# Third mixer: the Gelu of the compressed features moved three beats back, a one-column exponent behind it, the second layer one beat back

## Chip, cores and metric

One core of one Trainium2 chip. The metric is the device time of one execution in microseconds (us), lower is better. Five engines run programs of their own and meet only through semaphores: TensorE (PE in the profile, its weight loads PEld), VectorE (DVE), ScalarE (ACT), GpSimd (POOL) and SyncE (SP, which issues most of the DMAs).

## The reference, cut to what matters

Three layers on a sequence of 256 tokens with 1024 features: two layers of one kind (gated feed-forward, mixer, gated feed-forward), then one of another kind (mixer, feed-forward). The change lies in the mixer of the last one. It has two branches, a chunked mLSTM and an attention with three parts (compressed, selected and window keys). The compressed part reduces keys and values to 15 blocks by a small two-layer network:

```python
def compress_blocks(kv, pe, w1, w2):
    ...
    blk = kv[:, :, idx] + pe
    flat = blk.reshape(B, G, ncmp, CMP_LEN * dh)
    return jax.nn.gelu(flat @ w1, approximate=False) @ w2
...
    kcmp = compress_blocks(kc_t, cmp_k_pe, cmp_k_w1, cmp_k_w2)
    vcmp = compress_blocks(vc_t, cmp_v_pe, cmp_v_w1, cmp_v_w2)
...
        pc = masked_softmax(jnp.einsum('bghqd,bgnd->bghqn', qb, kc) * scale, cmask)
        o_cmp = jnp.einsum('bghqn,bgnd->bghqd', pc.astype(vc.dtype), vc)
```

The other two parts are ordinary softmax attention over 256 keys; with 8 heads they make 16 jobs, taken as 8 pairs.

## The kernel before

Everything is one straight program per engine, written out by hand. Weights stream from HBM through a ring of 8 raw buffers. ScalarE copies each weight tile into a high part (`whi`, line 1380), VectorE subtracts to get the low part (`wlo`, line 1989), and TensorE multiplies high and low parts separately to keep float32 accuracy; these products are most of the work.

The mixer of the last layer (`mixer2`, one function of that name in each engine's program) puts its small work between the big products. A counter, the beat, goes up after each block of big products; every engine has a function `tick` that raises its own counter and says which small steps are due at that beat. Nothing keeps the engines at the same beat but the semaphores, and each engine works strictly in the order of its program. Beats 31 to 38 lie between the blocks of the value projection of the mLSTM (tiles Mmv0, Mmv2, Mmv4, Mmv6, two beats each), beats 39 to 46 between those of the next projection (Mmo0 to Mmo6). On TensorE each of these blocks is lines 770, 771 and 775. Ahead of every second beat ScalarE and VectorE split the tiles that come next (`ahead`); how many tiles ahead is a table (`HI_LEAD`: two tiles, Mmo0 and Mmo2, fall due on ScalarE ahead of beat 35).

The steps around the change, with their lines:

- Attention pair 0 (the 16 jobs' first two) runs its scores at beat 29, its probabilities are turned at beats 33 and 34 (TensorE `turn_p`, line 1040; ScalarE copies each turned tile out of the one PSUM bank that they share, `turned_p`, line 1609, and the next turn waits for that copy). Pair 1 has its scores at beat 35 (TensorE line 1027), the row maxima on VectorE (lines 2234, 2235 and 2241) and four exponents on ScalarE at beat 35 (lines 1601 and 1602), and is turned at beats 39 and 40.
- The compressed part has steps of its own in `compressed`. TensorE step 0 (beat 31, line 1227) turns the first layer's sums, and ScalarE's step 1 applies Gelu to them (line 1810, out: `hc`, semaphore `c_hc`). TensorE step 1 (lines 1233 and 1236) is the second layer; it waits for `c_hc` and raises `c_w2`. ScalarE step 2 copies the results out in three pieces (lines 1680, 1681, 1816); it waits for `c_w2` and for two buffers that GpSimd clears (`vz`, line 2809 the second), and raises `c_kv` to 3. TensorE step 2 (line 1242, beat 36) waits for `c_kv` 3 and repeats the values for VectorE (line 2452). Step 3 on TensorE is at beat 38, line 1248; ScalarE's copy of the finished value projection is line 1942.
- GpSimd runs the mLSTM's small convolutions (lines 2790, 2793, 2795); ScalarE takes a Tanh of each when it is done (`conv_end`, line 1829, beats 32, 36, 40, 44).

An activation function needs its table in ScalarE. Where the next function is not in the table that is loaded, the compiled program has an ACT_TABLE_LOAD ahead of the instruction, under the same line number. Line 1534 is a one-column Gelu that an earlier author put ahead of the last feed-forward; it writes one column of `small` that nobody reads.

Of the kernel before, what the change touches and what calls it, by code (L numbers as in the profile page):

```python
# [10 lines left out]
ACT = mybir.ActivationFunctionType  # L11
# [404 lines left out]
def build_program(nc, x_in, wstream, gains, const_in, par_in, out, cat, pat, plan, addends):  # L416
# [3 lines left out]
    with ExitStack() as ctx:  # L420
        def sb(name, cols, dt=F32, parts=P):
            return ctx.enter_context(nc.sbuf_tensor(name, [parts, cols], dt))
# [17 lines left out]
        small = sb("small", 560)  # L440
# [7 lines left out]
        mhalf = small[:, 160:176]  # L448
# [250 lines left out]
        def pe_program(E):  # L699
            e = E.e  # L700
# [478 lines left out]
            def mixer2(s):  # L1179
                js = jobs2()  # L1180
                beat = 0

                def turn_k(a, first):
                    bk, dup = side[a], arena[:, a * 1024:a * 1024 + 1024]
                    if first:
                        E.wait_ge("x", 4 * (s - 1) + a + 1)
                        E.wait_ge("rp_add", 8 + a + 1)
                        turn4([dup[:, (2 + i) * P:(3 + i) * P] for i in range(4)], bk).then_inc(sem["kT_t"], 1)
                    else:
                        E.wait_ge("k3_ev", 2 * a + 2)  # L1190
                        E.wait_ge("kT_ev", a + 1)
                        turn4([dup[:, j * P:(j + 1) * P] for j in (0, 1, 6, 7)], bk).then_inc(sem["kT_t"], 1)

                def turn_q(a):
                    E.wait_ge("rp_add", 10 + a + 1)
                    E.wait_ge("kc2_ev", 4 * a + 4)
                    turn4([ro[:, a * 512 + c * P:a * 512 + c * P + P] for c in range(4)], side[a]).then_inc(sem["qkt_t"], 1)
# [23 lines left out]
                def compressed(step):  # L1221
                    b = side[3] if step < 4 else side[2]
                    if step == 0:
                        E.wait_ge("c_part", 1)
                        E.wait_ge("c_fold", 1)
                        for i in range(4):
                            ins = e.matmul(b[:, i * 30:i * 30 + 30], hpart[:, i * P:i * P + P], fold[:, 0:30], start=True, stop=True)
                        ins.then_inc(sem["c_hT"], 1)
                    if step == 1:
                        E.wait_ge("c_hc", 1)  # L1230
                        E.wait_ge("ld_p", 16)
                        for hb_ in range(2):
                            e.matmul(b[:, 0:30], PR("kw2")[:, hb_ * P:hb_ * P + P], hc[:, hb_ * 30:hb_ * 30 + 30], start=hb_ == 0, stop=hb_ == 1)
                        for g in range(2):
                            for hb_ in range(2):
                                ins = e.matmul(b[0:15, 64 + g * 64:128 + g * 64], hc[:, (2 + hb_) * 30 + g * 15:(2 + hb_) * 30 + g * 15 + 15],
                                               PR("vw2")[:, hb_ * P:hb_ * P + 64], start=hb_ == 0, stop=hb_ == 1)
                        ins.then_inc(sem["c_w2"], 1)
                    if step == 2:
                        E.wait_ge("c_kv", 3)  # L1240
                        for g in range(2):
                            ins = e.matmul(b[:, 256:320], C("rep")[:, g * P:g * P + P], vcs[:, g * 64:g * 64 + 64], start=g == 0, stop=g == 1)
                        ins.then_inc(sem["c_rep"], 1)
                    if step == 3:
                        E.wait_ge("c_v", 1)
                        for a in range(2):
                            for c in range(4):
                                ins = e.matmul(b[:, (a * 4 + c) * 32:(a * 4 + c) * 32 + 30], qT2[:, c * S + a * P:c * S + a * P + P],
                                               kcT[:, c // 2 * 30:c // 2 * 30 + 30], start=True, stop=True)
                        ins.then_inc(sem["c_sc"], 1)  # L1250
                    if step == 4:
                        E.wait_ge("c_s", 11)
                        E.wait_ge("pT_ev", 20)
                        for a in range(2):
                            ins = e.transpose(b[:, a * P:a * P + P], Pc[:, a * P:a * P + P], ident)
                        ins.then_inc(sem["c_pT"], 1)
# [46 lines left out]
                def tick():  # L1303
                    nonlocal beat
                    beat += 1
                    if 10 <= beat <= 13:
                        turn_k(beat % 2, beat < 12)
                    if beat in (24, 25):
                        turn_q(beat - 24)
                    if beat == 16:  # L1310
                        gate_rows()
                    attention(2, beat, 29, js, before)
                    if beat in (31, 34, 36, 38, 44):
                        compressed((31, 34, 36, 38, 44).index(beat))
                    if beat in range(ML, ML + 24, 6):
                        mlstm_scores((beat - ML) // 6)
                    if beat in range(ML + 4, ML + 28, 6):
                        mlstm_out((beat - ML - 4) // 6)
                    if beat in (ML + 28, ML + 30):
                        mlstm_turn((beat - ML - 28) // 2)  # L1320
# [35 lines left out]
        def act_program(E):  # L1356
            e = E.e
# [410 lines left out]
            def mixer2(s):  # L1768
                js = jobs2()
                beat = 0  # L1770
# [31 lines left out]
                def compressed(step):  # L1802
                    b = side[3] if step < 3 else side[2]
                    if step == 0:
                        E.wait_ge("tile", DONE["Mvw13"])
                        E.wait_ge("X", 8)
                        e.activation(hpart, side[3][:, :], ACT.Copy).then_inc(sem["c_part"], 1)
                    if step == 1:
                        E.wait_ge("c_hT", 1)
                        e.activation(hc, b[:, 0:120], ACT.Gelu).then_inc(sem["c_hc"], 1)  # L1810
                    if step == 2:
                        E.wait_ge("c_w2", 1)
                        E.wait_ge("vz", 2)
                        split_heads("c_kv", [kcT.rearrange("p (g hp n) -> p hp g n", g=2, hp=2)[:, hp] for hp in range(2)],
                                    b[:, 0:30].rearrange("p (g n) -> p g n", g=2))
                        e.activation(vcs[0:15, :], b[0:15, 64:192], ACT.Copy).then_inc(sem["c_kv"], 1)
                    if step == 3:
                        E.wait_ge("c_s", 5)
                        p3 = Pc.rearrange("p (r n) -> p r n", n=16)[:, :, 0:15]
                        e.activation(p3, p3, ACT.Exp).then_inc(sem["c_exp"], 1)  # L1820
                    if step == 4:
                        E.wait_ge("c_pT", 1)
                        e.activation(PcT, b[:, 0:S], ACT.Copy).then_inc(sem["c_pTe"], 1)
# [33 lines left out]
                def tick():  # L1857
                    nonlocal beat
                    beat += 1
                    if 10 <= beat <= 13:  # L1860
                        turned_k(beat % 2, beat < 12)
                    if beat == 18:
                        logf()
                    if beat in (24, 25):
                        turned_q(beat - 24)
                    if beat == 26:
                        exp_m()
                    if beat in CONV:
                        conv_end(CONV.index(beat))
                    if beat == 28:  # L1870
                        compressed(0)
                    attention(2, beat, 29, js)
                    if beat in (31, 34):
                        compressed((31, 34).index(beat) + 1)
                    if beat == 40:
                        compressed(3)
                    if beat == 44:
                        compressed(4)
                    if beat == ML + 1:
                        mlstm_exp(0)  # L1880
                    if beat in range(ML + 6, ML + 24, 6):
                        mlstm_exp((beat - ML) // 6)
                    if beat in (ML + 6, ML + 12, ML + 18, ML + 22):
                        mlstm_squares((ML + 6, ML + 12, ML + 18, ML + 22).index(beat))
                    if beat in (ML + 28, ML + 30):
                        mlstm_turned((beat - ML - 28) // 2)
# [1123 lines left out]
```

## Time and profile before

| | |
|---|---|
| median of 3 runs | 1405.89 us (1405.52 to 1406.15) |
| the profiled execution's own time | 1405.38 us |
| its span in the trace | 1403.6 us |
| TensorE busy | 1398.1 us |
| VectorE busy | 1087.4 us |
| ScalarE busy | 861.8 us |
| GpSimd busy | 229.0 us |

The span is from the first to the last instruction of the profiled execution; its own time has some 1.8 us around that. Busy times overlap between engines. Line numbers (L1810) are those of the kernel before.

### The profile page before, as it was taken

The numbers are of one execution on the slowest core, as the hardware profiler recorded it, in microseconds if no ns is written. First come the engines' busy times: TensorE is split into PE (matmuls) and PEld (weight loads), VectorE is DVE, ScalarE is ACT, GpSimd is POOL, SyncE is SP. The second block draws the span as 40 slices with busy tenths as digits, with TensorE's granted clock in tenths as the row PEclk, the third lists the DMA queues.
The fourth block names the chain that finished last, engine by engine and source line by source line (L and its number), as shares of the span: only waits on it lengthen the run. The fifth ranks groups of instructions, "written<-read, shape, count | busy, mean of one in ns | idle before, by whom it ended". The sixth has DMA issues, their size and how long they took to land.

```text
span 1403.6 us, 20147 instructions
## 1 busy us (share of the span) xinstructions
PE 1398.1 (100%) x7616; PEld 1194.2 (85%) x7616; DVE 1087.4 (77%) x1633; ACT 861.8 (61%) x1397; POOL 229.0 (16%) x307
## 2 busy tenths in 40 slices
PE   9999999999999999999999999999999999999999
PEld 7888888898888888888888888888888899888887
DVE  7878876776978878788775778788777878678776
ACT  6657656755667657676567646666567765455553
POOL 1112133000111001112050001114149200100000
PEclk9999999999999999999999999999999999999999
DMA  9999755354999759998564457999547336456551
GB/s 368 306 298 279 222 204 173 136 200 180 306 256 291 210 189 303 270 278 217 195 223 150 167 181 270 266 276 260 187 155 250 126 121 219 159 169 220 194 182 58
DMA packets 86328, 305.76 MB, mean 218 GB/s; under 512 B 11468, under 2 KB 11608, under 8 KB 86232
## 3 DMA queue, kind: packets, MB, share of 16 engines
q1 hardware_dynamic: 72120, 253.35, 50.5%
q0 software_dynamic: 13824, 50.34, 18.7%
q8 instruction: 61, 1.00, 0.3%
q10 hardware_dynamic: 288, 0.79, 0.1%
q14 instruction: 35, 0.29, 0.1%
HBM read 303.38 MB, written 1.06 MB: 217 GB/s over the span
## 4 chain that ended last, share of the span: by engine, by line
PE 95%; POOL 3%; DVE 1%; ACT 1%; issue 0%; ACTq 0%; POOLq 0%; DVEq 0%
PE bank L749 18%; PE bank L756 9%; PE bank L703 9%; PE bank L704 9%; PE bank L705 9%; PE bank L928 5%; PE bank L927 5%; PE bank L931 5%; PE bank L770 3%; PE bank L775 3%; PE bank L771 3%; PE bank L733 3%; PE bank L740 3%; PE bank L734 3%; PE bank L723 1%; PE bank L1055 1%
## 5 line engine op out<-in xcount | busy, mean ns | idle before, releaser
L1989 DVE TENSOR_TENSOR wlo<-raw,whi 128x1024 fp32r<-128x1024 f32 x409 | 492.5, 1232 | 12.2 <-ACT whi L1380 12.2
L1380 ACT ACTIVATE whi<-raw 128x1024 fp32r<-128x1024 f32 x409 | 417.4, 1048 | 19.2 <-PE bank L705 12.5
L749 PE MATMUL bank<-hx,whi 128*128 128x512 f32 x1088 | 268.6, 393 | 0.0
L749 PEld LDWEIGHTS bank<-hx,whi 128*128 128x128 f32 x1088 | 200.4, 188 | 41.3 <-issue 2.0
L703 PE MATMUL bank<-whi,hid 128*128 128x512 f32 x536 | 211.1, 394 | 0.0
L704 PE MATMUL bank<-wlo,hid 128*128 128x512 f32 x536 | 209.2, 390 | 0.0
L705 PE MATMUL bank<-whi,hid 128*128 128x512 f32 x536 | 208.8, 389 | 0.0
L756 PEld LDWEIGHTS bank<-hx,wlo 128*128 128x128 f32 x1088 | 143.0, 191 | 7.7
L756 PE MATMUL bank<-hx,wlo 128*128 128x256 f32 x1088 | 145.3, 282 | 0.0
L1989 DVE TENSOR_TENSOR wlo<-gates,whi 128x1024 fp32r<-128x1024 f32 x96 | 115.9, 1220 | 6.0 <-ACT whi L1380 5.5
L705 PEld LDWEIGHTS bank<-whi,hid 128*128 128x128 f32 x536 | 100.6, 188 | 21.4
L1380 ACT ACTIVATE whi<-gates 128x1024 fp32r<-128x1024 f32 x96 | 100.5, 1056 | 27.0 <-PE bank L705 14.3
L703 PEld LDWEIGHTS bank<-whi,hid 128*128 128x128 f32 x536 | 100.8, 188 | 18.9
L704 PEld LDWEIGHTS bank<-wlo,hid 128*128 128x128 f32 x536 | 100.9, 188 | 18.4
L1409 ACT ACTIVATE hid<-prod 128x256 fp32r<-128x256 f32 x78 | 32.6, 418 | 122.0 <-DVE prod L2299 58.6
L2696 POOL DMA_DIRECT2D gates<-w_dram x64 | 55.8, 872 | 288.2 <-DVE wlo L1989 288.0
L770 PE MATMUL bank<-whi,hx 128*128 128x512 f32 (+1 forms) x252 | 100.1, 398 | 0.0
L771 PE MATMUL bank<-whi,hx 128*128 128x512 f32 (+1 forms) x252 | 96.5, 384 | 0.0
L2651 POOL TENSOR_SCALAR small<-small 128x1 f32<-128x1 f32 x15 | 10.9, 725 | 403.8 <-ACT arena L1395 403.8
L775 PE MATMUL bank<-wlo,hx 128*128 128x512 f32 (+1 forms) x252 | 76.0, 384 | 0.0
L927 PE MATMUL bank<-whi,yhi 128*128 128x512 f32 x192 | 75.2, 392 | 0.0
L928 PE MATMUL bank<-whi,ylo 128*128 128x512 f32 x192 | 74.9, 390 | 0.0
(296 smaller groups left out, 2369.8 us busy)
## 6 DMA issues: line engine op xcount, KB each, us to landing
raw<-w_dram SPq DMA_DIRECT2D x414, 512.0 KB, 4.5
gates<-w_dram POOLq DMA_DIRECT2D x64, 512.0 KB, 7.9
gates<-w_dram SPq DMA_DIRECT2D x32, 512.0 KB, 5.7
arena<-w_dram POOLq DMA_DIRECT2D x32, 512.0 KB, 8.9
arena<-w_dram SPq DMA_DIRECT2D x16, 512.0 KB, 5.2
gain<-g_dram SPq DMA_DIRECT2D x7, 512.0 KB, 3.3
arena<-c_dram SPq DMA_DIRECT2D x2, 768.0 KB, 6.1
out_dram<-x SPq DMA_DIRECT2D x4, 256.0 KB, 2.0
```

What stands on the lines that cost most here:

```text
L703: e.matmul(psum, shi, mhi, start=first, stop=False, skip_group_check=True)
L704: e.matmul(psum, shi, mlo, start=False, stop=False, skip_group_check=True)
L705: return e.matmul(psum, slo, mhi, start=False, stop=last, skip_group_check=True)
L749: e.matmul(b[:, :], hi_of(j)[:, k * P:k * P + P], hx[:, k * 2 * S:k * 2 * S + 2 * S], start=k == 0, stop=False, skip_group_check=True)
L756: ins = e.matmul(b[:, 0:S], lo_of(j)[:, k * P:k * P + P], hiT(k), start=False, stop=k == KD - 1, skip_group_check=True)
L770: e.matmul(b[:, 0:n], hiT(k, a * P, a * P + P), w, start=k == 0, stop=False, skip_group_check=True)
L771: e.matmul(b[:, 0:n], loT(k, a * P, a * P + P), w, start=False, stop=False, skip_group_check=True)
L775: ins = e.matmul(b[:, 0:n], hiT(k, a * P, a * P + P), w, start=False, stop=k == KD - 1, skip_group_check=True)
L927: e.matmul(b[:, :], sh(k), half(hi_of(j), k), start=k == 0 and n not in (2, 4), stop=False, skip_group_check=True)
L928: e.matmul(b[:, :], sl(k), half(hi_of(j), k), start=False, stop=False, skip_group_check=True)
L1380: e.activation(hi_of(t), raw_of(t), ACT.Copy).then_inc(sem["w_hi"], 1)
L1989: e.tensor_tensor(lo_of(t), raw_of(t), hi_of(t).bitcast(F32), ALU.subtract).then_inc(sem["w_lo"], 1)
```

## The change

ScalarE's Gelu moves from beat 31 to beat 34, behind that beat's copy of a turned tile. Behind it stands a new exponent of one column into the same unread column of `small`. ScalarE's step 2 (three copies) moves from beat 34 to beat 35; in `tick` it stands behind the call of `attention`, so behind that beat's four exponents. TensorE's step 1 (the second layer) moves from beat 34 to beat 35, behind the scores of pair 1. TensorE's step 2 stays at beat 36, and so do all later steps.

```diff
@@ TensorE, mixer2, tick @@
                     attention(2, beat, 29, js, before)
-                    if beat in (31, 34, 36, 38, 44):
-                        compressed((31, 34, 36, 38, 44).index(beat))
+                    if beat in (31, 35, 36, 38, 44):
+                        compressed((31, 35, 36, 38, 44).index(beat))
@@ ScalarE, mixer2, compressed @@
                     if step == 1:
                         E.wait_ge("c_hT", 1)
                         e.activation(hc, b[:, 0:120], ACT.Gelu).then_inc(sem["c_hc"], 1)
+                        e.activation(small[:, 12:13], mhalf[:, 0:1], ACT.Exp)
@@ ScalarE, mixer2, tick @@
                     attention(2, beat, 29, js)
-                    if beat in (31, 34):
-                        compressed((31, 34).index(beat) + 1)
+                    if beat in (34, 35):
+                        compressed(beat - 33)
```

## Rows read from the trace of the kernel before

**Rows 1.** The page: span, and busy time of each engine.
```profile
span 1403.6 us, 20147 instructions
...
PE 1398.1 (100%) x7616; PEld 1194.2 (85%) x7616; DVE 1087.4 (77%) x1633; ACT 861.8 (61%) x1397; POOL 229.0 (16%) x307
```

**Rows 2.** Waits of TensorE over the span: us in total, times, longest.
```profile
PE bank L1344 <- POOL arena L2823: 1.0, 1, 1.0
PE bank L1040 <- ACT arena L1609: 0.5, 1, 0.5
```

**Rows 3.** Windows: length, busy us (instructions) of each engine, PEclk, DMA, GB/s.
```profile
1070.00:1078.00 8.00, 7.85 (x46) 6.47 (x45) 7.86 (x18) 6.69 (x16) 7.45 (x9) 1.00 0.77 280
...
1086.00:1092.00 6.00, 5.49 (x36) 4.59 (x35) 5.93 (x10) 5.63 (x15) 5.60 (x7) 1.00 0.53 178
```

**Rows 4.** Timeline of TensorE, beats 33 to 40: start us, duration us.
```profile
1074.90 0.62 PE L775 MATMUL bank<-wlo,hx 128*128 128x512 f32 x2
1075.36 0.49 PE L1040 MATMUL bank<-cst,arena 128*128 128x128 f32 x3
...
1076.61 0.63 PE L775 MATMUL bank<-wlo,hx 128*128 128x512 f32 x2
1077.39 0.52 PE L1040 MATMUL bank<-cst,arena 128*128 128x128 f32 x3
1077.74 0.53 PE L1233 MATMUL bank<-small,par 128*128 128x30 f32 x4
...
1078.75 0.50 PE L770 MATMUL bank<-whi,hx 128*128 128x512 f32 x1
...
1080.35 0.93 PE L1027 MATMUL bank<-arena 64*128 64x128 f32 x8
...
1082.69 0.55 PE L1242 MATMUL bank<-small,cst 128*128 128x64 f32 x4
...
1090.33 0.62 PE L775 MATMUL bank<-wlo,hx 128*128 128x512 f32 x2
1091.47 0.52 PE L1040 MATMUL bank<-cst,arena 128*128 128x128 f32 x3 [0.52 <-ACT arena L1609]
```

**Rows 5.** Timeline of ScalarE, the same stretch; in brackets the idle time before.
```profile
1074.05 1.28 ACT L1810 ACT_TABLE_LOAD   x1
1075.34 0.27 ACT L1810 ACTIVATE small<-bank 128x120 f32<-128x120 f32 x1
...
1076.76 0.48 ACT L1609 ACTIVATE arena<-bank 128x384 f32<-128x384 f32 x1
1077.95 0.49 ACT L1609 ACTIVATE arena<-bank 128x384 f32<-128x384 f32 x1 [0.70 <-PE bank L1040]
1081.64 0.19 ACT L1680 ACTIVATE arena<-bank 64x30 f32<-64x30 f32 x1 [3.21 <-POOL arena L2809]
...
1082.08 0.27 ACT L1816 ACTIVATE small<-bank 15x128 f32<-15x128 f32 x1
1082.25 1.99 ACT L1380 ACTIVATE whi<-raw 128x1024 fp32r<-128x1024 f32 x2
1084.26 1.28 ACT L1601 ACT_TABLE_LOAD   x1
1085.56 0.49 ACT L1601 ACTIVATE arena<-arena,small 128x128 f32<-128x128 f32 x1
...
1087.69 0.40 ACT L1829 ACTIVATE arena<-arena 128x256 f32<-128x256 f32 x1
...
1090.85 0.47 ACT L1609 ACTIVATE arena<-bank 128x384 f32<-128x384 f32 x1
```

**Rows 6.** Groups by line and form, ScalarE: count, busy us, mean ns.
```profile
L1534 ACT ACTIVATE small<-small 128x1 f32<-128x1 f32 x1 | 0.2, 203 | 0.0
```

**Rows 7.** Timeline of GpSimd: the end of the first convolution.
```profile
1073.54 0.74 POOL L2795 TENSOR_TENSOR arena<-arena 128x256 f32<-128x256 f32 x1
```

**Rows 8.** Timeline of VectorE: the last maximum of pair 1.
```profile
1082.78 0.25 DVE L2241 TENSOR_TENSOR small<-small 128x2 f32<-128x2 f32 x1
```

## The prediction

> **What bounds the kernel now.** The page first: TensorE is busy 1398.1 us of a span of 1403.6 [rows 1], so whatever TensorE waits longer or shorter shows in the time almost one for one, and the other engines matter only where they make it wait. Then TensorE's waits over the span: four in all, 2.1 us, the longest 1.0 us at the very start; in the stretch of the change there is one, 0.5 us, a turn of attention probabilities (L1040) waiting for ScalarE to empty the bank (L1609) [rows 2]. The windows agree: TensorE lacks 0.15 us in 1070 to 1078 and 0.51 us in 1086 to 1092, at a granted clock of 1.00 [rows 3]. So there is little to win here, and a new wait would have no slack to hide in. Last the timelines of TensorE and ScalarE across beats 33 to 40 [rows 4, 5]; the sum is made from them.
>
> What can be won is read by starts, since the ends of matmuls are modelled. From the last L775 of a block to the turn behind it is 0.46 us where nothing waits (1074.90 to 1075.36). At beat 34 it is 0.78 (1076.61 to 1077.39), at beat 40 it is 1.14 (1090.33 to 1091.47) [rows 4]. That is 0.32 + 0.68 = 1.00 us lost to ScalarE's late copies. The first comes from the Gelu: its table load and the function stand at 1074.05 to 1075.61, ahead of the copy that the turn waits for. The second comes from the load of the exponent's table, which stands at 1084.26 ahead of pair 1's exponents and pushes everything on ScalarE behind it [rows 5].
>
> **The change part by part.** No work is removed. The number of table loads stays two: today Gelu's at beat 31 and the exponent's at beat 35; then both at beat 34. Added is one exponent of one column, for which the one-column Gelu stands, 0.20 us [rows 6]. TensorE issues the same matmuls, with L1233 and L1236 one beat later; their price, about 1.0 us (1077.74 to 1078.75 [rows 4]), moves and does not change. No DMA moves, and no step on SP or GpSimd.
>
> *Beat 33 and 34.* Without the Gelu ScalarE does the Tanh L1829 as soon as GpSimd's convolution ends, 1073.54 + 0.74 = 1074.28 [rows 7], then one split of 1.0 us and is free at about 1075.8. The turn that starts at 1075.36 is out by about 1075.9 (a copy starts 0.56 us behind its turn: 1077.39 to 1077.95), its copy ends at 1076.4, and the turn of beat 34 goes at 1076.61 + 0.46 = 1077.07 instead of 1077.39 [rows 4, 5]. Gain 0.32 us. If ScalarE were late even so, the gain is nothing; I take all of it.
>
> *ScalarE from there.* The copy L1609 runs 1077.63 to 1078.12. Then Gelu's load; from the start of a load to its function is 1.29 us, the function 0.27, so Gelu ends at 1079.70. The exponent's load starts 0.02 later, the one-column exponent at 1081.01; the next small instruction follows about 0.22 behind (1081.64 to 1082.08 is two such steps), 1081.23. Then the two splits that beat 35 has ahead of it, L1380 x2, 1.9 us to the next start (1.99 less an overlap of about 0.1), 1083.13. Then pair 1's four exponents, now without a load, 2.13 us (1085.56 to 1087.69), 1085.26. They are not late for their maxima: these come 2.68 us behind the scores (1080.35 to 1083.03 [rows 4, 8]), which makes 1081.6. And only then, because the step stands behind the attention of beat 35, the three copies of step 2, 0.44 + 0.27 us: `c_kv` is complete at 1085.97 [rows 5].
>
> *TensorE meanwhile.* From 1077.07 it has the same work up to step 2 as before, so it arrives at L1242 at about 1082.69 - 0.32 = 1082.37. On the way the second layer waits for Gelu, over at 1079.70; TensorE is there at 1077.07 + 0.35 + (1080.35 - 1078.75) + 0.93 = 1079.95 (0.35 for the turn, 1077.39 to 1077.74; 0.93 for the scores), so it waits a tenth at most, which the next wait swallows. Today the copies that L1242 needs end at 1082.35, held by GpSimd's clearing of their buffer, just in time. With the change they end at 1085.97; with the 0.15 us that the wait of beat 40 shows between ScalarE's end (1090.85 + 0.47) and TensorE's start (1091.47), L1242 goes at 1086.12 [rows 4, 5]. **TensorE stands for 3.75 us.** Queued behind it are the blocks of Mmv6 and everything after them; VectorE, whose L2452 waits for L1242, stands too, and then keeps the distance to TensorE that it has today.
>
> *Beat 39 and 40.* ScalarE is now 1.1 us earlier by the clock and TensorE 3.4 later, so ScalarE waits for TensorE and empties the bank in time. The turn of beat 40 goes at 1086.12 + (1090.33 + 0.46 - 1082.69) = 1094.22, against 1091.47: the loss of 0.68 is gone too. **The sum is 3.75 - 0.32 - 0.68 = 2.75 us.** Behind beat 40 TensorE waits for nothing until the end of the mixer [rows 2], and what others hold ready for it they hold ready earlier; I cost that at nothing. Bounds: the gain at beat 34 can fail (+0.32), each of the ten or so handovers in ScalarE's chain can be off by a tenth (0.6 either way), and if a weight tile were late the splits would be (they followed at once before, so I leave it at +0.5). The sum lies between 2.0 and 3.6 us.
>
> A word on the loads. The rows show the function 1.29 us after the start of its load of 1.28, and a load 0.02 us after the instruction ahead of it [rows 5]; there is no further price of a switch. The Trainium skill (ScalarE: Activation LUTs, "What ACT_TABLE_LOAD costs") gives a switch about 2.66 us, 1.38 of it for draining beside the load itself. By that figure two switches in ScalarE's chain would lengthen it by 2.8 us, and the sum would be about 5.5 us. The rows of this trace do not show that part, and the measurement decides.
>
> **The rivals.** *Faster.* If ScalarE had the copies of step 2 ready when TensorE comes to beat 36, only the two gains would be left: -1.00 us, 1404.9. For that they would have to end by 1082.2, 3.75 us earlier than worked out; the three copies would have to go ahead of the splits and the four exponents (4.0 us together). The order of the program speaks against it; it holds only if I read that order wrongly. *Half a wait.* ScalarE's chain is shorter, because an item of it does not stand where I put it: if the two splits fell before the Gelu, or the exponent's load were not placed with the one-column exponent, the wait would be 1.8 to 2.5 us and the sum 0.8 to 1.5, some 1407. *The clock.* 3.75 us would be TensorE's longest stand, and the granted clock, 1.00 in both windows [rows 3], could fall to the lower of its two levels, 1.2 instead of 2.4 GHz, behind it. Each block of big products takes 1.4 to 1.6 us at the full clock (1075.36 to 1077.07 less the turn's 0.35; 1078.75 to 1080.35 [rows 4]), and would take that again at half; one or two blocks give 4.2 to 6 us in all, 1410 to 1412. For it speaks the length, against it that the longest wait seen so far, 1.0 us, left no mark. The Trainium skill (TensorE: Matmul & The Clock Gate, "HAM oscillation") states just this, that the clock is halved when TensorE idles for its data, and the next work starts cold; no row here shows it. *The longer chain* of the page on loads, 5.5 us or 1411.4, I give almost nothing, for the rows above.
>
> **How the numbers follow.** The sum is made against the profiled execution, 1405.38 us: 1408.1. That execution lies 0.51 us under the median, 1405.89; against the median the same 2.75 us give 1408.6. A measurement of this kernel tells about 0.2%, 2.8 us, from no change, so the likeliest case lies almost on that bound. Chances: the likeliest case, 2.0 to 3.6 us (1407.9 to 1409.5), 0.72; the clock or a longer chain 0.14; half a wait 0.08; faster 0.06. Of the likeliest case a little under half (0.49) lies beyond 2.8 us: slower 0.72 x 0.49 + 0.14 = 0.49. The faster case is worth 1.0 us, 0.07%, and counts as the same unless more is won than I see; I leave it 0.02 for that: faster 0.02, same 0.72 x 0.51 + 0.08 + 0.04 = 0.49. The range leaves out the faster case and the far ends of the other two: 1406.9 to 1410.5.
>
> **What would show it.** Right: TensorE's waits gain one of 3.4 to 4 us at L1242 on ScalarE's L1816, and lose the one of L1040; ScalarE's timeline has two loads with only Gelu between them, then two L1380, four exponents without a load, then L1680, L1681, L1816; VectorE's L2452 stands as long. Wrong: copies of L1816 ahead of the exponents, no wait at L1242, a granted clock under 1.00 between 1086 and 1096, or a new wait behind beat 40.

## The result, and the profile after

The changed kernel takes 1410.12 us (median of 10 runs, 1408.35 to 1411.75) against 1405.89 (10 runs, 1405.52 to 1406.20): ratio 1.0028, 95% interval 1.0020 to 1.0037, so +4.2 us, slower. The time was forecast at 1408.6, with a range from 1406.9 to 1410.5. The spread is part of the result: the kernel before stays within 0.7 us, the changed one does not. Three of its runs lie between 1408.35 and 1408.59, at a granted clock of 1.000 over the whole span; seven lie between 1409.79 and 1411.75, at 0.998 or 0.999.

The page of the profiled execution (1410.28 us) has the same work in a longer span; TensorE's busy time has hardly moved [rows 1].

```profile
span 1408.5 us, 20148 instructions
...
PE 1398.8 (99%) x7616; PEld 1194.5 (85%) x7616; DVE 1086.2 (77%) x1633; ACT 862.7 (61%) x1398; POOL 228.5 (16%) x307
```

TensorE's waits of the changed kernel (us in total, times, longest): the wait of L1040 [rows 2] is gone, and there is one for the last of ScalarE's copies, L1817 (L1816 before). The 1.5 us at L723 are at the start of the program, in the first layer's normalization; they differ from profile to profile and come back below.

```profile
PE bank L1242 <- ACT small L1817: 3.3, 1, 3.3
PE bank L723 <- DVE arena L2008: 1.5, 1, 1.5
```

TensorE's timeline, beats 33 to 45, to be held against [rows 4]. This execution comes to beat 33 0.80 us later than the one before (1076.16 against 1075.36), so only distances are compared.

```profile
1076.16 0.49 PE L1040 MATMUL bank<-cst,arena 128*128 128x128 f32 x3
...
1077.88 0.49 PE L1040 MATMUL bank<-cst,arena 128*128 128x128 f32 x3
...
1079.69 0.93 PE L1027 MATMUL bank<-arena 64*128 64x128 f32 x8
1080.55 0.63 PE L1233 MATMUL bank<-small,par 128*128 128x30 f32 x4
...
1082.69 0.62 PE L775 MATMUL bank<-wlo,hx 128*128 128x512 f32 x2
1086.65 1.12 PE L1242 MATMUL bank<-small,cst 128*128 128x64 f32 x4 [3.34 <-ACT small L1817]
...
1088.10 0.63 PE L771 MATMUL bank<-whi,hx 128*128 128x512 f32 x1
...
1094.68 0.49 PE L1040 MATMUL bank<-cst,arena 128*128 128x128 f32 x3
...
1096.40 0.49 PE L1040 MATMUL bank<-cst,arena 128*128 128x128 f32 x3
...
1106.70 0.67 PE L1278 MATMUL bank<-arena,gates 128*128 128x256 f32 x2
```

The two turns of beats 33 and 34 are 1.72 us apart instead of 2.03: the first stand is gone. From the last L775 of a block to what follows is 0.46, so TensorE was ready for L1242 at 1083.15 and stood 3.50 us (the view of waits counts 3.34 of it, from the modelled end of the last product). What comes next was not in the sum: L771 takes 0.63 us, where the same line takes 0.39 to 0.40 before the stand. The windows of the changed kernel show why (length, busy us of each engine, granted clock, DMA share, GB/s):

```profile
1083.00:1086.60 3.60, 0.31 (x2) 0.00 (x0) 0.00 (x0) 3.55 (x13) 3.28 (x6) 0.99 0.30 5
1086.60:1090.10 3.50, 3.45 (x10) 2.95 (x11) 2.30 (x3) 2.19 (x3) 3.26 (x5) 0.52 0.02 7
1090.10:1096.00 5.90, 5.90 (x37) 5.13 (x36) 5.83 (x10) 1.99 (x4) 5.51 (x6) 1.00 0.58 179
```

TensorE stood for 3.5 us; for the next 3.5 us the granted clock was at 0.52, about the lower of its two levels (1.2 instead of 2.4 GHz), then at 1.00 again. From L1242 to the turn of beat 39 that makes 8.03 us (1086.65 to 1094.68).

ScalarE's timeline, to be held against [rows 5]:

```profile
1078.40 0.49 ACT L1609 ACTIVATE arena<-bank 128x384 f32<-128x384 f32 x1 [1.23 <-PE bank L1040]
1078.91 1.28 ACT L1810 ACT_TABLE_LOAD   x1
1080.20 0.27 ACT L1810 ACTIVATE small<-bank 128x120 f32<-128x120 f32 x1
1080.49 1.28 ACT L1811 ACT_TABLE_LOAD   x1
1081.79 0.20 ACT L1811 ACTIVATE small<-small 128x1 f32<-128x1 f32 x1
1081.90 1.99 ACT L1380 ACTIVATE whi<-raw 128x1024 fp32r<-128x1024 f32 x2
1083.79 0.48 ACT L1601 ACTIVATE arena<-arena,small 128x128 f32<-128x128 f32 x1
...
1085.91 0.17 ACT L1680 ACTIVATE arena<-bank 64x30 f32<-64x30 f32 x1
...
1086.33 0.27 ACT L1817 ACTIVATE small<-bank 15x128 f32<-15x128 f32 x1
```

The order is the one worked out: copy of the turned tile, two loads with Gelu between them, two splits, four exponents without a load, and only then the three copies. ScalarE hardly idles from 1078.40 to 1086.60; TensorE waits for the end of that queue. The loads again have no price behind their 1.28 us: functions start 1.29 and 1.30 us after them. The drain that the Trainium skill adds (ScalarE: Activation LUTs, "What ACT_TABLE_LOAD costs") does not show here either.

### The profile page after: what moved, and what is told of

Read it like the earlier page. It is cut to its first block, busy times and chain, and to the rows that moved or that the text cites. A ratio compares the mean times of both kernels' runs of the same rounds, so it can differ in the third digit from the quotient of the medians.

```text
span 1408.5 us, 20148 instructions
## 1 busy us (share of the span) xinstructions
PE 1398.8 (99%) x7616; PEld 1194.5 (85%) x7616; DVE 1086.2 (77%) x1633; ACT 862.7 (61%) x1398; POOL 228.5 (16%) x307
## 4 chain that ended last, share of the span: by engine, by line
PE 98%; ACT 1%; DVE 1%; DMA 0%; issue 0%; SPq 0%; DVEq 0%; ACTq 0%
PE bank L749 18%; PE bank L756 9%; PE bank L703 9%; PE bank L704 9%; PE bank L705 9%; PE bank L927 5%; PE bank L928 5%; PE bank L931 5%; PE bank L770 4%; PE bank L775 4%; PE bank L771 4%; PE bank L733 3%; PE bank L740 3%; PE bank L734 3%; PE bank L723 1%; PE bank L1027 1%
## 5 line engine op out<-in xcount | busy, mean ns | idle before, releaser
L771 PE MATMUL bank<-whi,hx 128*128 128x512 f32 (+1 forms) x252 | 96.9, 386 | 0.0
L775 PE MATMUL bank<-wlo,hx 128*128 128x512 f32 (+1 forms) x252 | 76.4, 386 | 0.0
```

What stands on the lines that cost most here:

```text
L771: e.matmul(b[:, 0:n], loT(k, a * P, a * P + P), w, start=False, stop=False, skip_group_check=True)
L775: ins = e.matmul(b[:, 0:n], hiT(k, a * P, a * P + P), w, start=False, stop=k == KD - 1, skip_group_check=True)
```

## The experiments

Times are medians; "before" is the kernel before, run beside them: 1405.89 us for the changed kernel, 1405.91 for the first four experiments, 1405.99 for the last three. A stand is counted by starts, as above. The granted clock is that of the whole span; 0.997 to 0.999 means that it fell for some us. Where it fell is shown only by a trace, of one run of each kernel; of the 48 runs of the kernel before that stand beside the experiments, none had a clock under 1.00.

| kernel | time, us | against before | ratio, 95% | stand at L1242 | runs with clock under 1.00 |
|---|---|---|---|---|---|
| changed | 1410.12 | +4.23 | 1.0020 to 1.0037 | 3.50 | 7 of 10 |
| copies ahead of the exponents | 1406.34 | +0.43 | 0.9994 to 1.0012 | 1.38 | 0 of 11 |
| the moves alone | 1407.35 | +1.44 | 1.0003 to 1.0021 | 1.82 | 3 of 11 |
| filled wait | 1408.41 | +2.50 | 1.0009 to 1.0027 | 3.50, of it 0.76 idle | 0 of 11 |
| longer wait | 1413.12 | +7.21 | 1.0039 to 1.0065 | 6.49 | 5 of 5 |
| no one-column exponent | 1410.58 | +4.59 | 1.0019 to 1.0044 | 3.40 | 5 of 5 |
| copies at beat 34 | 1405.41 | -0.58 | 0.9986 to 1.0004 | 0.05 | 0 of 11 |
| exponent alone, at beat 34 | 1406.06 | +0.07 | 0.9992 to 1.0009 | none | 0 of 11 |

**Copies ahead of the exponents.**

```diff
-                    attention(2, beat, 29, js)
-                    if beat in (34, 35):
-                        compressed(beat - 33)
+                    if beat == 35:
+                        compressed(2)
+                    attention(2, beat, 29, js)
+                    if beat == 34:
+                        compressed(1)
```

> As the changed kernel, but ScalarE's three copies of step 2 stand ahead of pair 1's exponents at beat 35. Theory (TensorE's stand at L1242 is the place of the copies in ScalarE's order; the clock falls only behind a long stand): the copies end 2.1 us sooner, the stand falls from 3.5 to 1.4 us, the clock stays at 1.00, sum 1.4 - 1.0 = +0.4 us, about 1406.3, with a narrow spread. Rival (the loss is Gelu and the table loads at beat 34, wherever the copies stand): like the changed kernel, 1408 to 1411 with its wide spread.

1406.34 us, 1406.01 to 1406.70. ScalarE's and TensorE's timelines of that kernel:

```profile
1081.63 1.99 ACT L1380 ACTIVATE whi<-raw 128x1024 fp32r<-128x1024 f32 x2
1083.53 0.17 ACT L1680 ACTIVATE arena<-bank 64x30 f32<-64x30 f32 x1
```
```profile
1082.42 0.62 PE L775 MATMUL bank<-wlo,hx 128*128 128x512 f32 x2
1084.26 0.66 PE L1242 MATMUL bank<-small,cst 128*128 128x64 f32 x4 [1.22 <-ACT small L1817]
...
1090.75 0.49 PE L1040 MATMUL bank<-cst,arena 128*128 128x128 f32 x3
```

Gelu and both loads stand where the change puts them, and all but a tenth of the loss is gone: it came from the copies' place behind the exponents. The stand is 2.12 us shorter, which is what the four exponents take in the changed kernel (1083.79 to 1085.91). From L1242 to the turn of beat 39 is 6.49 us here, against 8.03 in the changed kernel's profile: the lower clock cost 1.54 us there.

**The moves alone.**

```diff
-                        e.activation(small[:, 12:13], mhalf[:, 0:1], ACT.Exp)
...
+                    if beat == 31:
+                        compressed(1)
                     attention(2, beat, 29, js)
-                    if beat in (34, 35):
-                        compressed(beat - 33)
+                    if beat == 35:
+                        compressed(2)
```

> The two moves of step 1 (TensorE) and step 2 (ScalarE) alone: Gelu stays at beat 31 and there is no one-column exponent. Theory: Gelu is out of the chain, the exponent's load is in it again ahead of pair 1's exponents; the copies end at about 1084.8 in the time of the kernel before, TensorE stands 2.2 us at L1242, the stand of beat 34 (0.32) stays and that of beat 40 (0.68) goes: +1.5 us, 1407.4, clock 1.00. Rival (Gelu's new place makes the loss): no wait at L1242, within 0.3 us of the kernel before.

1407.35 us. TensorE's and ScalarE's timelines of that kernel:

```profile
1082.99 0.62 PE L775 MATMUL bank<-wlo,hx 128*128 128x512 f32 x2
1085.27 0.66 PE L1242 MATMUL bank<-small,cst 128*128 128x64 f32 x4 [1.66 <-ACT small L1816]
```
```profile
1081.10 1.28 ACT L1601 ACT_TABLE_LOAD   x1
```

Gelu was never in the chain, and TensorE still stands. The turns of beats 33 and 34 are 2.03 us apart as in the kernel before (1076.12 to 1078.15), so the stand there stays with Gelu at beat 31. The stand at L1242 was 0.4 us shorter than I had worked out. ScalarE did not wait for the maxima of pair 1: its first exponent starts at 1082.40, right behind the table load, and needs only the maximum of the first job (over at 1082.11); the last one is over at 1082.86. Not expected: three of the eleven runs had a clock of 0.999 and took 1408.36 to 1409.11, the eight others 1406.83 to 1407.58.

**Filled wait.** The added products go into the bank in which the turned tiles lay.

```diff
                     if step == 2:
+                        E.wait_ge("pT_ev", 18)
+                        for i in range(3):
+                            e.matmul(side[2][:, :], ident, cst[:, 0:512], start=True, stop=True)
                         E.wait_ge("c_kv", 3)
```

> As the changed kernel, but TensorE runs three plain float32 products of 128x512 that nobody uses into a free bank ahead of its wait for the copies, about 2.7 us in all, so that it idles less than 1 us. Theory (the changed kernel's runs above 1409 are those in which the clock fell behind the stand): every run near the changed kernel's lowest, 1408.4, granted clock 1.00 in all. Rival (the spread comes from elsewhere, the start or the DMAs): 1408.4 to 1411.8 as before, or longer by what the added products cost.

1408.41 us, 1407.88 to 1409.05, where the changed kernel's three runs at full clock take 1408.35 to 1408.59. TensorE's timeline and windows of that kernel (lines shifted by three; L1242 are the added products, L1245 is the old L1242):

```profile
1083.17 2.73 PE L1242 MATMUL bank<-cst 128*128 128x512 f32 x6
1086.67 0.66 PE L1245 MATMUL bank<-small,cst 128*128 128x64 f32 x4 [0.76 <-ACT small L1820]
```
```profile
1086.60:1090.00 3.40, 3.33 (x18) 2.84 (x18) 2.63 (x3) 2.81 (x5) 3.24 (x4) 1.00 0.01 2
```

The copies come no sooner; work without use in the wait holds the clock at 1.00 and takes 1.7 us off the median. This separates the two parts of the loss: 2.5 us are the stand less the two gains, the rest is the clock.

**Longer wait.**

```diff
                         e.activation(small[:, 12:13], mhalf[:, 0:1], ACT.Exp)
+                        e.activation(small[:, 13:14], mhalf[:, 0:1], ACT.Gelu)
+                        e.activation(small[:, 14:15], mhalf[:, 0:1], ACT.Exp)
```

> As the changed kernel, with a second one-column Gelu and a second one-column exponent behind the first, so two more table loads in ScalarE's chain at beat 34. Theory: the chain is 2 x (1.29 + 0.2) = 3.0 us longer and TensorE's stand at L1242 goes from 3.5 to 6.5 us; and the clock falls in every run, which adds the 1.6 us of the profiled changed run or more: 1408.4 + 3.0 + 1.6 = 1413.0 or above, with no run under 1412. Rival (the loads are hidden, the stand has another cause): 1410 as the changed kernel.

1413.12 us, 1412.77 to 1413.72. TensorE's wait and the windows of that kernel:

```profile
1082.09 0.62 PE L775 MATMUL bank<-wlo,hx 128*128 128x512 f32 x2
1089.04 1.12 PE L1242 MATMUL bank<-small,cst 128*128 128x64 f32 x4 [6.33 <-ACT small L1819]
```
```profile
1089.00:1092.00 3.00, 2.96 (x9) 2.57 (x10) 1.80 (x2) 2.19 (x3) 2.75 (x4) 0.50 0.02 5
1092.00:1094.40 2.40, 2.40 (x7) 1.82 (x7) 2.36 (x4) 0.60 (x1) 2.32 (x2) 0.50 0.43 121
```

Two more loads with their functions lengthen the stand by 2.99 us and the clock falls in all five runs. In this one it is at 0.50 for all of the 5.4 us shown behind the stand, where the changed kernel had 0.52 for 3.5 us.

**No one-column exponent.**

```diff
-                        e.activation(small[:, 12:13], mhalf[:, 0:1], ACT.Exp)
```

> The changed kernel without the one-column exponent. The exponent's load then stands ahead of pair 1's exponents instead of behind Gelu, still in the same chain ahead of the copies. Theory: TensorE's stand at L1242 is 0.1 to 0.2 us shorter, 3.3 us, and the spread stays that of the changed kernel: runs from 1408.2 to 1411.5, part of them with a granted clock under 1.00. Rival (the one-column exponent and its load are what costs): 1.3 us or more below the changed kernel.

1410.58 us, 1409.70 to 1411.19: the stand is 0.10 us shorter, the time is within the changed kernel's spread. ScalarE's and TensorE's timelines of that kernel:

```profile
1081.92 1.28 ACT L1601 ACT_TABLE_LOAD   x1
```
```profile
1086.09 0.66 PE L1242 MATMUL bank<-small,cst 128*128 128x64 f32 x4 [3.24 <-ACT small L1816]
```

The load only changes its place in the same queue. So the second condition of the prediction's "half a wait", a load that is not placed with the one-column exponent, does not shorten the stand. The clock fell in all five runs, so the low end that I expected, 1408.2, did not occur.

**Copies at beat 34.** The version that the runs point to: Gelu late, the second layer at beat 35, and the copies ahead of ScalarE's splits.

```diff
                     attention(2, beat, 29, js)
-                    if beat in (34, 35):
-                        compressed(beat - 33)
+                    if beat == 34:
+                        compressed(1)
+                        compressed(2)
```

> As the changed kernel, but ScalarE's three copies of step 2 stand at beat 34, right behind Gelu and the one-column exponent, so ahead of the two splits and of pair 1's exponents. Theory: ScalarE waits there, in time that it has, for the second layer and for GpSimd's clearing (over at 1081.6 in the time of the kernel before); the copies end at 1082.35, TensorE stands 0.1 us at L1242, and the stands of beats 34 and 40 (0.32 and 0.68) are gone: -0.9 us, 1405.0, clock 1.00. Rival (the splits and exponents come later and something behind them makes TensorE wait): 1405.9 or above.

1405.41 us, 1405.02 to 1405.73, against 1405.99: 0.58 us less, not told from no change by the interval, and less than the 0.9 expected. TensorE's timelines, of the kernel before and of this one, beats 40 to 45:

```profile
1101.46 0.49 PE L1040 MATMUL bank<-cst,arena 128*128 128x128 f32 x3
1101.80 0.67 PE L1278 MATMUL bank<-arena,gates 128*128 128x256 f32 x2
```
```profile
1083.15 0.66 PE L1242 MATMUL bank<-small,cst 128*128 128x64 f32 x4
...
1091.36 0.49 PE L1040 MATMUL bank<-cst,arena 128*128 128x128 f32 x3
...
1101.31 0.49 PE L1040 MATMUL bank<-cst,arena 128*128 128x128 f32 x3
1102.06 0.67 PE L1278 MATMUL bank<-arena,gates 128*128 128x256 f32 x2 [0.27 <-issue]
```

The stand at L1242 is 0.05 us by starts, and there is none at beats 34 and 40. But at beat 45 the mLSTM's first product, L1278, follows its turn by 0.75 us instead of 0.34: 0.41 us of the gain is given back there. From the first turn of beat 33 L1278 comes after 25.95 us (1076.11 to 1102.06) instead of 26.44, so 0.49 us is kept up to there.

**The exponent alone, at beat 34,** in the kernel before:

```diff
-                    if beat in (31, 34):
-                        compressed((31, 34).index(beat) + 1)
+                    if beat == 31:
+                        compressed(1)
+                    if beat == 34:
+                        e.activation(small[:, 12:13], mhalf[:, 0:1], ACT.Exp)
+                        compressed(2)
```

> The kernel before with the one-column exponent alone, at beat 34 ahead of ScalarE's step 2, where ScalarE stood 3.21 us; Gelu stays at beat 31 and no step moves. Theory: the exponent's load goes into that idle time, the exponents of pair 1 end 1.3 us sooner, the stand of beat 40 (0.68) goes and that of beat 34 (0.32) stays: -0.7 us, 1405.2. Rival (the late copies of beat 40 have another cause): 1405.9.

1406.06 us: no gain, which I had not expected. TensorE's and VectorE's rows of the kernel before, then TensorE's, VectorE's and GpSimd's of this one:

```profile
1089.08 0.49 PE L1040 MATMUL bank<-cst,arena 128*128 128x128 f32 x3
```
```profile
1100.84 0.86 DVE L2489 SCALAR_TENSOR_TENSOR gates<-arena 64x256 f32<-64x256 f32 x2
```

```profile
1089.84 0.49 PE L1040 MATMUL bank<-cst,arena 128*128 128x128 f32 x3
...
1091.56 0.49 PE L1040 MATMUL bank<-cst,arena 128*128 128x128 f32 x3
...
1101.70 0.55 PE L1040 MATMUL bank<-cst,arena 128*128 128x128 f32 x3
1102.52 0.67 PE L1278 MATMUL bank<-arena,gates 128*128 128x256 f32 x2 [0.28 <-issue]
```
```profile
1096.61 0.72 DVE L2244 TENSOR_TENSOR small<-small 128x2 f32<-128x2 f32 x1
...
1100.97 0.67 DVE L2256 TENSOR_SCALAR arena<-arena,small 128x128 f32<-128x128 f32 x2
1101.56 0.86 DVE L2492 SCALAR_TENSOR_TENSOR gates<-arena 64x256 f32<-64x256 f32 x2
```
```profile
1096.57 0.74 POOL L2798 TENSOR_TENSOR arena<-arena 128x256 f32<-128x256 f32 x1
```

The stand of beat 40 is gone: the turns are 1.72 us apart instead of 2.39 (1089.08 to 1091.47 [rows 4]). At beat 45 all of it is given back. The turn starts at 1101.70, behind VectorE's L2256 (over at 1101.64), and L1278 at 1102.52, behind VectorE's L2492 (over at 1102.42), which prepares its operand. From the first turn of beat 33 L1278 comes after 26.42 us (1076.10 to 1102.52), in the kernel before after 26.44 (1075.36 to 1101.80). So there, at beat 45, VectorE's queue is a second bound, right behind the one that I had seen: in the kernel before, too, L1278 starts 0.10 us behind the instruction that prepares its operand (L2489, over at 1101.70).

VectorE did not simply keep its old times, though. Counted from the first turn of beat 33, it comes to the first maxima of the next pair 0.52 us sooner than in the kernel before (19.84 us, at 1095.94, against 20.36, at 1095.72). It loses this in one small instruction behind them: L2244, of 128x2, takes 0.72 us, in the kernel before 0.16 (L2241 at 1096.40), and ends 0.02 us behind a GpSimd instruction beside which it ran (L2798, over at 1097.31). With the copies at beat 34 the same instruction takes 0.55 and 0.23 us for the two jobs, each time ending 0.02 us behind one of GpSimd's. That GpSimd held it up is read from these times alone; no run moved GpSimd's step. That VectorE's or GpSimd's order could be mended so that the gain stays was not tried.

## Why the prediction was right, and where it was not

*The stand at L1242* was the main mechanism, and it came as worked out: behind the same queue, in the order given. The term was 3.75 us and measured 3.50. Of the difference, 0.11 is the step behind the one-column exponent (0.11 us instead of 0.22), 0.10 the handover to TensorE (0.05 instead of 0.15), 0.04 the start of the copy behind its turn. That the copies' place makes the stand is shown by the run with the copies ahead of the exponents.

*The two gains* came too: 0.31 us at beat 34 and 0.67 at beat 40, against 0.32 and 0.68. Their causes are shown too: with Gelu back at beat 31 the stand of beat 34 stays, and with the exponent's load in idle time the stand of beat 40 goes. Both gains hold in the changed kernel: TensorE is late there, and VectorE has caught up before beat 45: it stood 1.88 us waiting for the scores of the next pair, against 0.47 in the kernel before (turn of beat 40 to L1278: 1096.40 to 1106.70 in the changed kernel, 10.30 us; 1091.47 to 1101.80 before, 10.33). Without the stand they are not all kept: 0.41 of the two gains is lost at beat 45 with the copies at beat 34, and all of the gain of beat 40 with the exponent alone. The sentence that TensorE waits for nothing behind beat 40 was true of the kernel before, and did not say by how little.

*The sum without the clock*, 2.75 us, measured 2.50 in the kernel with the filled wait, and 2.46 to 2.70 in the changed kernel's three runs at full clock.

*The clock* is where the prediction went wrong in size. It put the clock at nothing in the sum and had it as a rival, with a chance of 0.14 together with a longer chain, against it "the longest wait seen so far, 1.0 us, left no mark"; it came in 7 of 10 runs and so set the median. A granted clock under 1.00 between 1086 and 1096 was one of its own signs of being wrong. The likeliest case ended at 1409.5; of the clock's rival, 1410 to 1412, the stated range took in only the first half us. That 1410.12 lies inside it is in part luck: the kernel without the one-column exponent, with almost the same stand, has its median at 1410.58. A wait of 1.0 us said nothing of one of 3.75, and rows for the longer one did not exist. The price of a fall, given as one or two blocks of 1.4 to 1.6 us, was about right: 1.54 us in the profiled run between L1242 and beat 39, and 1.2 to 3.4 us by the runs above those at full clock. The Trainium skill (TensorE: Matmul & The Clock Gate, "HAM oscillation") had named this for a stand on data. The traces agree, with 0.52 behind a stand of 3.5 us, but three of the ten runs kept the full clock.

The profiled run's ledger from beat 33 to beat 45 (L1040 to L1278, 30.54 us against 26.44): -0.31 + 3.50 + 1.54 - 0.67, and 0.04 of small differences, make +4.10. The span grew by 4.9; the other 0.80 lies ahead of beat 33. Of it 0.71 is there at the first L723 already (7.82 us against 7.11), where this execution has a wait that the one before has not. That wait was 0.3 to 1.5 us in the profiles of the other kernels here, and stands over 1000 us ahead of the first step that was changed.

## What to carry to other kernels

Where engines run hand-ordered queues, moving a step by one beat is a move past everything that stands between on that engine; list it by name and add its time before counting what the move saves. A wait of a few us on a busy TensorE can cost more than its length, because the clock may fall behind it; ask for the wait's length first. If the wait can't go, work that nobody needs may keep the clock up, as it did here in 11 of 11 runs. A gain of a few tenths at one wait holds only if the next engine in line has that much slack: look for the next handover that starts just in time, and for what its engine will run beside when it comes sooner.

## What the hardware showed that was not expected

By the granted clock of the whole span, the fall of the clock is a matter of chance at middle lengths: after an idling of 0.76 and a stand of 1.38 us in none of 11 runs each, of 1.82 us in 3 of 11, of 3.40 and 3.50 us in 12 of 15, of 6.49 us in 5 of 5. So the changed kernel has runs up to 3.4 us apart. Only one run of each kernel has a trace; that the clock fell at the stand or right behind it is shown there, for 3.40, 3.50 and 6.49 us, and taken for the other runs.

GpSimd was faster while VectorE stood: in the changed kernel four instructions of the convolution in a row (L2794 and L2796 twice, 1083.92 to 1086.83) took 0.61, 0.73, 0.61 and 0.72 us. In the kernel before the same four, beside a working VectorE, took 0.61, 0.74, 1.47 and 1.59 us (L2793 and L2795, 1083.11 to 1087.76). With the slow L2244 above, that makes cases in both directions; what the two engines share is not shown here.
